# A fused two-block transformer kernel: relative bias planes read with a skew out of device memory, and 16 early expert blocks for 12 in the first layer

## What is computed

```python
x = x + gate1 * mix
h2 = rms_norm(x, norm2_g[l]) * (1.0 + scale2) + shift2
x = x + gate2 * peer_ffn(h2, peer_wq[l], peer_keys[l], peer_u[l], peer_v[l])

def peer_ffn(h, w_q, sub_keys, expert_u, expert_v):
    # q = h @ w_q: 8 heads, two halves of 128; scores against 2 x 128 keys
    # top 16 of each half, top 16 of their sums: 16 experts of 16384 a head and token
    # gate = softmax of the 16 sums
    # y = sum over experts of gate * gelu(h . u_e) * v_e
```

```python
def _t5_bucket(rel):            # 32 buckets of the distance q - k, logarithmic from 16 on
rel = q_pos[:, None] - k_pos[None, :]
bias = jnp.transpose(table[_t5_bucket(rel)], (2, 0, 1))   # 8 planes of 256 x 256
s = einsum(q, k) * scale + bias, and -1e30 where rel < 0
```

## Time and profile before

| | us |
|---|---|
| median of three runs | 3033.38 |
| the profiled execution | 3034.02 |
| its span | 3032.2 |
| TensorE busy | 2937.6 (97%) |
| DVE busy | 1970.5 (65%) |
| ACT busy | 1308.6 (43%) |
| layer 0 of the first block, from start to the gate stage | 283.5 |
| its gate stage | 88.5 |
| its early combines and regular blocks | 371.7 to 1066 |

### The profile page before, as it was taken

The page is one execution under the profiler, slowest core; times in us unless marked ns, Lnnn a source line. Parts: engine busy times, 40 slices in busy tenths (PEclk is TensorE's granted clock), DMA queues, the critical chain, the costliest instruction groups (busy, mean ns, idle before and its releaser), DMA issues.

```text
span 3032.2 us, 49210 instructions
## 1 busy us (share of the span) xinstructions
PE 2937.6 (97%) x17378; PEld 2555.9 (84%) x17378; DVE 1970.5 (65%) x3639; ACT 1308.6 (43%) x2110; POOL 274.5 (9%) x398
## 2 busy tenths in 40 slices
PE   8899999999999999999999999998999999999999
PEld 4686989999999876887999999998977888878897
DVE  4759966777777633898666666666556654655664
ACT  1245834444444412575444444444443433533433
POOL 0026700000000000572000000000000000000000
PEclk9899999999999998999999999999999999999999
DMA  8542256666666641404555555554334454324454
GB/s 327 197 157 84 72 187 235 226 235 232 227 234 230 206 155 56 167 8 128 192 186 186 198 191 194 190 194 176 125 120 168 171 185 172 147 112 160 153 181 153
DMA packets 130815, 524.41 MB, mean 173 GB/s; under 512 B 17981, under 2 KB 28093, under 8 KB 108025
## 3 DMA queue, kind: packets, MB, share of 16 engines
q1 hardware_dynamic: 120648, 508.13, 48.4%
q10 hardware_dynamic: 10034, 14.52, 1.4%
HBM read 519.44 MB, written 3.16 MB: 172 GB/s over the span
## 4 chain that ended last, share of the span: by engine, by line
PE 86%; DVE 7%; ACT 4%; issue 1%; DVEq 1%; DMA 1%; ACTq 0%; POOL 0%; SPq 0%
PE acc L1390 23%; PE prob_ps L1378 21%; PE acc L1014 7%; PE acc L1603 6%; PE acc L1616 6%; PE acc L999 3%; PE acc L973 2%; PE acc L1550 2%; PE acc L1360 2%; PE turn_ps L1122 2%; PE acc L952 2%; PE prob_ps L1341 2%; PE acc L1575 1%; PE acc L1096 1%; PE acc L1253 1%
## 5 line engine op out<-in xcount | busy, mean ns | idle before, releaser
L1378 PEld LDWEIGHTS prob_ps<-hTr,utr 128*128 128x128 f32 x5472 | 686.3, 191 | 19.6 <-issue 2.0
L1378 PE MATMUL prob_ps<-hTr,utr 128*128 128x256 f32 x5472 | 692.3, 283 | 1.3 <-issue 1.1
L1390 PE MATMUL acc<-vr,wtr 128*128 128x512 f32 x2736 | 663.6, 391 | 0.2 <-DVE vr L2776 0.2
L1390 PEld LDWEIGHTS acc<-vr,wtr 128*128 128x128 f32 x2736 | 499.3, 188 | 94.9 <-issue 0.6
L2776 DVE TENSOR_TENSOR vr<-slab,vr 128x1024 fp32r<-128x1024 f32 x228 | 279.3, 1225 | 357.9 <-ACT vr L2036 357.9
L2036 ACT CAST vr<-slab 128x1024 fp32r<-128x1024 f32 x228 | 239.5, 1050 | 524.1 <-PE acc L1390 524.0
L2751 DVE TENSOR_TENSOR utr<-slab,utr 128x1024 fp32r<-128x1024 f32 x228 | 277.9, 1219 | 16.1 <-ACT utr L2003 16.1
L2305 POOL TENSOR_TENSOR small<-small 128x1 f32<-128x1 f32 (+4 forms) x29 | 26.2, 902 | 2610.3 <-DVE small L2368 1410.5
L2003 ACT CAST utr<-slab 128x1024 fp32r<-128x1024 f32 x228 | 238.6, 1047 | 16.6 <-DMA slab<-in_peer_u 10.5
L3032 DVE TENSOR_TENSOR slab_lo<-slab,w_hi 128x2048 fp32r<-128x2048 f32 x64 | 143.8, 2288 | 123.0 <-ACT w_hi L2271 123.0
L2271 ACT CAST w_hi<-slab 128x2048 fp32r<-128x2048 f32 x64 | 119.3, 1907 | 158.5 <-DMA slab<-in_pack_b 150.6
(11 more groups left out here) (314 smaller groups left out, 4415.4 us busy)
## 6 DMA issues: line engine op xcount, KB each, us to landing
slab<-in_pack_b SPq DMA_DIRECT2D x132, 1024.0 KB, 4.8
slab<-in_peer_v SPq DMA_DIRECT2D x256, 512.0 KB, 3.5
slab<-in_peer_u SPq DMA_DIRECT2D x244, 512.0 KB, 4.5
arena<-in_pack_a SPq DMA_DIRECT2D x84, 512.0 KB, 4.8
slab<-in_pack_a SPq DMA_DIRECT2D x40, 1024.0 KB, 6.9
arena<-in_peer_u SPq DMA_DIRECT2D x6, 1024.0 KB, 15.1
slab<-in_pack_b SPq DMA_DIRECT2D x4, 832.0 KB, 5.6
arena<-in_pack_a SPq DMA_DIRECT2D x2, 1024.0 KB, 18.6
```

The source lines that it names most:

```text
L1378: ins = pe.matmul(prob_ps[:, m % 2, 0:S], utr[:, m % 2, uh, k * P:k * P + P], hTr[:, hh, k, :], start=(k == 0 and n == 0), stop=(k == KD - ...
L1390: ins = pe.matmul(y_ps[:, t, n, :], wtr[:, m % 2, wh, t * P:t * P + P], v[:, vh, n * 512:n * 512 + 512], start=first and k == 0, stop=last ...
```

## The change

The row of 511 biases is now written 128 times, once for each query of a tile (`spread(t5row, 1, P)`, 8 x 128 x 512 numbers, 2 MB for 16 KB). The causal mask becomes a second matmul into the same row (`ones` by a mask row of 255). With 128 copies, the skewed read can step back one number from row to row: a step of 511 numbers over rows of 512. So SP copies the planes from `t5_dram` straight to `bias_dram`, in 16 transfers within device memory. Flip, mask matmuls, ACT's copies and its store go. `first_blocks` goes ahead of the transfers in SP's queue. In layer 0, 16 blocks are early for 12, and 7 stand before the gate stage for 3. ACT waits for the row's write (t5_out) before the gate stage and for the 16 copies in layer 1.

```diff
-EARLY = (12, 16)
+EARLY = (16, 16)
 LISTED = (0, 12)
-AHEAD = (3, 12)
+AHEAD = (7, 12)
...
-        t5_dram = nc.dram_tensor("t5_rows", [8, 512], F32).ap()
+        t5_dram = nc.dram_tensor("t5_rows", [8, P, 512], F32).ap()
...
                     if name == "wq3":
+                        first_blocks(0)
                         sp.wait_ge(t5_out, 16)
+                        sp.sem_inc(passed["sp"], 1)
                         for h in range(8):
                             for t in range(T):
-                                sp.dma_start(skewed[:, h, t, :],
-                                             bass.AP(t5_dram.tensor, h * 512 + (P if t == 0 else 0), [[1, P], [1, S]]))\
-                                    .then_inc(t5_skew, 16)
-                        first_blocks(0)
+                                first = h * P * 512 + (255 if t == 0 else 127)
+                                sp.dma_start(bias_dram[:, (h * T + t) * S:(h * T + t + 1) * S],
+                                             bass.AP(t5_dram.tensor, first, [[511, P], [1, S]])).then_inc(t5_saved, 16)
...
-                        pe.wait_ge(t5_in, 64)
-                        pe.matmul(prob_ps[0:8, 0, :], relb[0:BUCKETS, :], onehot[0:BUCKETS, :], start=True, stop=True)\
+                        pe.wait_ge(t5_in, 48)
+                        pe.matmul(prob_ps[0:8, 0, :], relb[0:BUCKETS, :], onehot[0:BUCKETS, :], start=True, stop=False)
+                        pe.matmul(prob_ps[0:8, 0, S:2 * S - 1], ones[0:1, 0:8], future[0:1, 1:S], start=False, stop=True)\
                             .then_inc(t5_row, 1)
                 if l == 0:
-                    pe.wait_ge(t5_skew, 16 * 16)
                     pe.wait_ge(t5_kept, 1)
-                    for h in range(8):
-                        if h >= 2:
-                            pe.wait_ge(t5_done, h - 1)
-                        pe.matmul(prob_ps[:, h % 2, :], flip, skewed[:, h].rearrange("p t s -> p (t s)"),
-                                  start=True, stop=False)
-                        pe.matmul(prob_ps[:, h % 2, :], ident[:], causal_a, start=False, stop=True).then_inc(t5_flip, 1)
-                    pe.wait_ge(t5_done, 8)
...
-                    load(t5_in, flip, io["k_flip"])
-                    load(t5_in, causal_a, io["k_causal"].rearrange("p t s -> p (t s)"))
+                    load(t5_in, future[0:1, :], io["k_causal"][0:1, 0, :])
...
-                        load(t5_out, t5_dram, t5row[0:8, :])
+                        load(t5_out, t5_dram, spread(t5row[0:8, :], 1, P))
...
                 if l == 0:
-                    for h in range(8):
-                        if h in (2, 4):
-                            candidates(PH - 3 + h // 2)
-                        act.wait_ge(t5_flip, h + 1)
-                        act.copy(skewed[:, h].rearrange("p t s -> p (t s)"), prob_ps[:, h % 2, :]).then_inc(t5_done, 1)
-                    act.wait_ge(t5_done, 8)
-                    load(t5_saved, bias_dram, skewed.rearrange("p h t s -> p (h t s)"))
+                    candidates(PH - 2)
+                    candidates(PH - 1)
...
                 if l == 0:
-                    act.wait_ge(t5_saved, 16)
+                    act.wait_ge(t5_out, 16)
...
                     load(pre_gain.sem, wpre, wide(io["norm_mix_pre_2"][0], D))
+                    act.wait_ge(t5_saved, 16 * 16)
```

More of the change, by code:

```diff
@@ L353, in two_blocks @@
         t5_out = sem("t5_out")
-        t5_skew = sem("t5_skew")
-        t5_flip = sem("t5_flip")
-        t5_done = sem("t5_done")
         t5_saved = sem("t5_saved")
@@ L589, in two_blocks @@
         r5 = Region(arena)
-        skewed = r5.take(8, T, S)
-        flip = r5.take(P)
         onehot = r5.take(512)
@@ L594, in two_blocks @@
         t5row = r5.take(512)
-        causal_a = r5.take(T * S)
+        future = r5.take(S)
         assert r5.at <= 8192
-        t5_dram = nc.dram_tensor("t5_rows", [8, 512], F32).ap()
+        t5_dram = nc.dram_tensor("t5_rows", [8, P, 512], F32).ap()
         bias_dram = nc.dram_tensor("bias_rows", [P, 8 * T * S], F32).ap()
@@ L3086, in constants @@
         "k_ident": np.eye(P, dtype=np.float32),
-        "k_flip": np.ascontiguousarray(np.eye(P, dtype=np.float32)[::-1]),
         "k_iota": np.broadcast_to(np.arange(P, dtype=np.float32), (P, P)).copy(),
```

## The result

The changed kernel took 3045.65 us (median of 10 runs, 3038.55 to 3051.93), the kernel before 3034.28 (10 runs, 3029.36 to 3045.9). The ratio is 1.0032, interval 1.0021 to 1.0043: some 10 us slower, within the 0.5% called no change. (The ratio is estimated over the executions together with its interval; the quotient of the medians is 1.0037.) The forecast was 3035.6, range 3024 to 3046: the median lies 0.35 us inside the upper end.

What follows compares the result with a forecast made beforehand. TensorE was taken as the bound (86% of the chain of waits). Later gates +11.2, lower clock +2.4, early blocks' saving -11.4 gave +2.2 us on 3034.02, or 3036.2; with the median 0.6 lower, 3035.6, range 3024 to 3046.

Steps and rivals of the forecast that it cites:

- No change by more than 0.5%: Whole kernel: +2.2 us forecast, with anything within 15 us counted as no change; chance 0.92.
- Rival D: Routing: issuing the 1024-piece DMA holds ACT at 193.7 us and delays DVE's chain; 3040 to 3050 us; chance 0.15.
- Rival E: Before block 0: device-memory copies run late, so the second conditioning piece slips beyond 268 us; 5 to 12 us; chance 0.05.
- three signs named for being wrong: Hole before block 0 under 8 us, ACT's DMA issue over 3 us, or gate-stage group no longer 2.65 us.
- Block 0 waits for ACT's copy behind the exponential: Before early block 0: TensorE idles about 14 us until ACT copies the conditioning piece; block 0 starts at 268.8 us.
- Seven blocks, turned pairs and the lower clock from block 0 to the gates: Layer 0 ahead of the gates: gates start 11.2 us later, at 294.7, plus 2.4 us for the lower clock.
- The gate stage keeps its length: Layer 0 gate stage: 64 early-block steps remain in it, so it keeps its 88.5 us.
- Sixteen combines, and four regular blocks fewer: After layer 0's gates: four more combines cost 11.07 us, four fewer regular blocks save 22.48; 11.4 us saved.
- so it costs nothing: The 2 MB bias write during routing: lands in 14 us, between 7 and 30, with 15 us to spare for SP.
- The issue on ACT: Routing on ACT: issuing the 2 MB write takes 1.5 to 2 us, at least 1.4 us of it hidden.
- Rival B: From block 0: the chip keeps its clock or regains it at once; -0.2 us, 3033.2; chance 0.10.
- rival C: Before block 0: ACT's copy does not hold it, so freed time is used; 11.4 us faster, 3022.0; chance 0.06.

Runs made afterwards that it cites:

- e2: Changed kernel with ACT copying the two late conditioning pieces before the exponential, which moves behind early block 3's gelu; layer 882.40 us against the changed kernel's 894.08.
- e1: Changed kernel with the 2 MB write starting from 128 partitions, 8 copies each, instead of 8 partitions; ratio 1.0004 to the kernel before, layer +1.4 us.
- e6: The e1 kernel plus 28 idle 128x256 matmuls behind the second conditioning piece; ratio 1.0014 to the kernel before, layer 1.2 us shorter than e1.
- e4: Changed kernel with 12 early blocks in layer 0, 3 ahead of the gates, as before; layer 4.8 us longer than in the kernel before.
- the two repairs: Changed kernel with both the write from 128 partitions and ACT's copies before the exponential; 0.44% under the kernel before, layer 876.13 us.
- e8: As e1, but the write reads partitions 0 to 31, 4 copies of each row, each written 32 times; write rate about 200 GB/s.

## Why the prediction was right and where it was not

- **No change by more than 0.5%**: right, but at +10 us for +2.2, and the range held with luck: its upper end is 0.35 us above the median, and its upper part was meant for rivals D and E, not for the 5.6 us that came (below). None of the three signs named for being wrong came (hole 9.18, issue 0.84, group 2.65 us), so they did not test the step that failed.
- **Block 0 waits for ACT's copy behind the exponential**: right, shown by e2, where moving the exponential closes the hole. In e1 it is 14.62 us for 14.8 forecast. In the changed kernel it is 9.18, because the first, unforeseen wait pushed TensorE's own work by 10.6 us and block 0 by only 5.2 (14.62 - 10.62 + 5.18).
- **Seven blocks, turned pairs and the lower clock from block 0 to the gates**: forecast 25.9 + 2.4 = 28.3 us; 291.10 - 262.83 = 28.27 after, 27.67 in e1. The clock's part, forecast 2.4, is seen in the first pair of blocks, which takes 7.14 us at granted clock 1.00: 9.46 in the changed kernel (2.3 more), 9.97 in its repetition (2.8), 8.80 in e1 (1.7). Of the holes of 0.35 us forecast, 0.1 to 0.2 came.
- **The gate stage keeps its length**: 88.14 us before and after.
- **Sixteen combines, and four regular blocks fewer**: 16 combines 45.79 us (forecast 45.68), regular blocks 5.62 each.
- **The step that failed** is the one that ends "so it costs nothing", on the write of 2 MB. It asked only when SP needs the result, and took 14 us of landing, from 7 to 30, by the row of a write from 128 partitions. Measured: 48 GB/s and about 47 us, so it was late even for SP, whose 29 us of room it had counted. And it left out what else moves in those microseconds: the slabs of wq3, the second of which TensorE needs 27 us after the write's issue. This is what cost: 5.6 us in the layer (after less e1), against 0 in the sum. The rule of the Trainium skill cited there, that size 8 in the slowest dimension uses at most 8 of the 16 engines, is borne out (at most 8 pieces under way, busy share 0.4), but by it the landing would have been twice 6.9 us; the write took more than three times that.
- **The issue on ACT** (0.31 us before, taken as 1.5 to 2): 0.84 us, hidden. Rival D is out. Rival E (copies late, second piece late): its condition came, a landing later than about 240 us (172.79 + 68.6 = 241.4 in the frame of the kernel before), but not its price of 5 to 12 us: TensorE does not wait for the second piece in the changed kernel's profiled run, 0.86 us in its repetition, 0.56 in e2 and 1.49 in e4. The copies' issue took 0.60 us each, their landing 2.9.
- Rival B, no loss of clock, is out by the granted clock of 0.50 and the slow first pair, which e6 takes away; rival C, no hole, is out for this kernel, and e2 makes it so by another order on ACT.
- **The rest of the 10 us**: 7.0 are in the layer. The other 3 or so are not explained. They lie in stretches that vary by 4 to 8 us between executions of one kernel; the shortest mixing stage of layer 1 with the new planes is 0.6 us longer than the longest without.

## What to carry over

Before a large DMA is costed at nothing because its reader is late, list every other transfer in the window in which it runs, with the time at which each is needed; and look at which partitions it reads, since few neighbouring partitions make a small source slow and long. Work taken from the engine that bounds the kernel arrives only as far as the next wait in another engine's program order: here one statement on ACT held 12 us, and the two repairs together turned +10 us into -10 (-10.9 to -12.0 in the layer). Extra early work is worth its full saving only where it fills time that the engine would have stood idle.

## What was not expected of the hardware

- The rate of a DMA out of SBUF by the partitions read: 48, 98, 200 and 380 GB/s (above), with the DMA engines 0.4 busy in the first two.
- A write at 48 GB/s slows others far beyond its bytes: two slabs of 1 MB landed after 9.3 and 23.1 us for 4.8 and 7.5, two loads of u of 0.5 MB after 12.4 for 4.8.
- A copy of 128 KB within device memory with a skew of one element a row: issue 0.60 us, landing 2.9 us in the changed kernel (3.2 to 3.8 in e1, e6 and e8).
- The issue of a DMA with 1024 pieces: 0.84 us from partitions 0 to 7, 0.73 from eight 16 apart, 0.69 from 0 to 31, 0.63 from 128.
